# A two-layer conv and attention decoder on one core: raw x transposed first, its norm applied later

## The chip, the cores and the metric

The kernel runs on one core of one Trainium2 chip. The metric is device time in microseconds (us) of one execution, lower is better. The core has TensorE (PE, matmuls), VectorE (DVE), ScalarE (ACT), GpSimd (POOL) and SyncE (SP, which here only issues DMAs). Each works through a program of its own in order, and they wait for one another by semaphores.

## The reference

For S = 256 tokens and D = 1024 features, in float32:

```python
h = rmsnorm(x, norm_mix[0])              # y = x * rsqrt(mean(x*x) + EPS);  h = y * weight per feature
bg, cg, xv = split(h @ a_w_in, 3)        # three projections of 1024 columns
x = x + (bg * causal_conv3(cg * xv)) @ a_w_out
x = x + conv_ffn(rmsnorm(x, norm_ffn[0]))            # (silu(conv(h @ w_gate) + b) * (h @ w_up)) @ w_down, width 2816
k, v = split(rmsnorm(x, kv_norm) @ w_kv, 2)
x = x + attention(rmsnorm(x, norm_mix[1]) @ w_q, k, v) @ w_o
x = x + conv_ffn(rmsnorm(x, norm_ffn[1]))
out = rmsnorm(x, final_norm)
```

The convolution works along the tokens, feature by feature. The rms factor of a token (called rstd below) is one number per token, the norm weight one number per feature.

## The kernel before

All matrices are streamed once. A **slot** is 1 MB of weights, [128, 2048] in SBUF: 256 output columns for all 8 blocks k of 128 input features. SP loads slot s into one of six `raw` buffers (`load`), ACT rounds it to a high part (`hi(s)`), DVE subtracts to get the low part (`lo(s)`), and PE multiplies. A product is hi*hi + hi*lo + lo*hi. In the usual form (`project`) the weights are stationary and the tokens move: 16 matmuls of 512 columns (`both`: the high weight against the high and low part of h) and 16 of 256 columns (`narrow`: the low weight against the high part). The result lies by feature, in `main` and `cross` halves of a PSUM pair; ACT copies `cross` (`mixer_cross`), DVE adds `main` (`a_whole_sum`), and PE may then reuse that pair.

Slots 0 and 1 of the first projection hold 256 columns of C and 256 of x (`cg`, `xv`), slots 2 and 3 the next 256 of each, up to slot 7; four slots of B follow, then four of the output matrix. For each pair of slots DVE multiplies C by x and runs three taps on two blocks (`conv_a(i)`); later it multiplies by B (`gate_a`).

Before the change the beginning runs thus. SP loads x by token halves (tokens 0 to 127 in two pieces, tokens 128 to 255 in one), then slot 0 in halves, then slot 1. ACT squares x, DVE and POOL form rstd (POOL by a power), DVE multiplies x by rstd and by the norm weight that PE has spread over the partitions (`normalise`), PE transposes (`transposes`), ACT and DVE make hi and lo of it (`h_hi`, `h_lo`). Slots 0 and 1 are multiplied in another form, with the tokens stationary (`first_rows`): 8 k x 3 parts x 2 token halves x 2 slots = 96 matmuls of 256 columns. Their result lies by token, so it is copied (`copy_opening`) and turned by 8 transposes (`turn_opening`) within slot 2. `warm(n)` issues n matmuls whose result is not used.

Everything from slot 4 on is the same in both kernels, but for line numbers, counts of semaphores, and what GpSimd is given (below).

## Time and profile before

| | |
|---|---|
| median of 3 runs | 587.63 us (587.48 to 587.85) |
| the profiled execution | 587.62 us, span of its records 585.8 us |
| PE busy | 577.2 us, 99% of the span |
| DVE, ACT, POOL busy | 420.3, 314.9, 10.1 us |
| PE's share of the chain that ended last | 93% |

The span runs from the first record to the last; some 1.8 us lie around it. Busy time is a sum over instructions; matmuls overlap, so the time of one matmul in a stream is read from the spacing of the starts, or from the chain that ended last, where a group stands with its total and its count. Prefixes: L950 is line 950 of the kernel; PEld is the load of stationary data.

### The profile page before, as it was taken

What the parts mean: (1) busy time and instruction counts of PE and PEld (TensorE: products, weight loads), DVE (VectorE), ACT (ScalarE), POOL (GpSimd) and SP (SyncE); (2) the same over time, 40 slices, a digit from 0 to 9 for tenths busy, and PEclk for the clock granted to TensorE, in tenths of its full rate; (3) what the DMA queues carried; (4) which work ended last, traced back from release to release, by engine and by line L of the source; (5) the groups of instructions that cost most, each with busy time, mean ns of one, the idle gap of its engine ahead of it and who ended that gap; (6) DMA issues with size and microseconds to landing.
All of it is one profiled execution on the core that took longest, in us unless ns stands there. A gap on an engine that the chain in (4) does not pass through costs nothing.

```text
span 585.8 us, 8105 instructions
## 1 busy us (share of the span) xinstructions
PE 577.2 (99%) x3119; PEld 499.0 (85%) x3119; DVE 420.3 (72%) x508; ACT 314.9 (54%) x380; POOL 10.1 (2%) x22
## 2 busy tenths in 40 slices
PE   8999999999999999999999999999999999999995
PEld 6988888888888888888888899888888888888884
DVE  4688877767667667766886788896786667667765
ACT  5534453567544554555545666645665544554541
POOL 2000000000000000000100000000000000000001
PEclk9999999999999999999999999999999999999999
DMA  8995667456655655556654644274546655654001
GB/s 276 345 320 161 218 215 238 142 182 210 216 186 175 216 190 175 185 172 212 215 180 142 254 139 146 75 255 170 173 160 213 216 191 173 212 199 160 1 0 73
DMA packets 80917, 108.08 MB, mean 185 GB/s; under 512 B 1833, under 2 KB 71665, under 8 KB 80882
## 3 DMA queue, kind: packets, MB, share of 16 engines
q1 hardware_dynamic: 80160, 104.97, 54.2%
q10 hardware_dynamic: 722, 2.63, 1.2%
q8 instruction: 25, 0.41, 0.3%
q14 instruction: 10, 0.08, 0.0%
HBM read 106.54 MB, written 1.05 MB: 184 GB/s over the span
## 4 chain that ended last, share of the span: by engine, by line
PE 93%; DVE 3%; ACT 2%; DMA 1%; issue 1%; POOL 0%; SPq 0%; DVEq 0%; ACTq 0%
PE pair L950 36%; PE pair L958 19%; PE acc L1005 7%; PE acc L1009 7%; PE acc L1007 7%; PE pair L932 3%; PE pair L934 3%; PE pair L933 3%; PE acc L933 1%; PE acc L934 1%; PE acc L932 1%; PE pair L1019 1%; DMA xs<-in_x 1%; DVE wgt L617 1%; ACT acc L377 1%
## 5 line engine op out<-in xcount | busy, mean ns | idle before, releaser
L617 DVE TENSOR_TENSOR wgt<-raw,wgt 128x2048 fp32r<-128x2048 f32 x94 | 214.7, 2289 | 53.1 <-ACT wgt L359 52.8
L950 PE MATMUL pair<-hA,wgt 128*128 128x512 f32 x864 | 206.0, 391 | 0.0
L359 ACT ACTIVATE wgt<-raw 128x2048 fp32r<-128x2048 f32 x94 | 179.4, 1911 | 24.3 <-PE acc L1009 20.9
L950 PEld LDWEIGHTS pair<-hA,wgt 128*128 128x128 f32 x864 | 159.9, 188 | 31.8
L958 PEld LDWEIGHTS pair<-hA,wgt 128*128 128x128 f32 x864 | 108.0, 191 | 2.6
L958 PE MATMUL pair<-hA,wgt 128*128 128x256 f32 x864 | 108.8, 283 | 0.0
L1005 PE MATMUL acc<-wgt,kq_hi 128*128 128x512 f32 x160 | 49.3, 389 | 0.0
L1007 PE MATMUL acc<-wgt,kq_hi 128*128 128x512 f32 x160 | 49.3, 389 | 0.0
L1009 PE MATMUL acc<-wgt,kq_lo 128*128 128x512 f32 x160 | 49.2, 389 | 0.0
L427 ACT ACTIVATE scratch<-scratch 128x512 f32<-128x512 f32 x22 | 13.9, 632 | 59.7 <-DVE scratch L695 59.7
L441 ACT ACTIVATE scratch<-pair 128x512 f32<-128x512 f32 x20 | 11.9, 594 | 58.3 <-PE pair L958 58.3
L716 DVE TENSOR_TENSOR scratch<-scratch,pair 128x512 f32<-128x512 f32 x20 | 13.7, 686 | 31.0 <-ACT scratch L441 31.0
L1005 PEld LDWEIGHTS acc<-wgt,kq_hi 128*128 128x128 f32 x160 | 30.0, 188 | 6.2
L1007 PEld LDWEIGHTS acc<-wgt,kq_hi 128*128 128x128 f32 x160 | 30.0, 188 | 6.2
L1009 PEld LDWEIGHTS acc<-wgt,kq_lo 128*128 128x128 f32 x160 | 30.0, 188 | 6.2
L932 PE MATMUL pair<-wgt,hA 128*128 128x512 f32 (+1 forms) x96 | 34.7, 361 | 0.6 <-DVE wgt L831 0.6
L934 PE MATMUL pair<-wgt,hA 128*128 128x512 f32 (+1 forms) x96 | 34.0, 354 | 0.0
L933 PE MATMUL pair<-wgt,hA 128*128 128x512 f32 (+1 forms) x96 | 34.0, 354 | 0.0
L695 DVE SCALAR_TENSOR_TENSOR scratch<-scratch,f_par 128x255 f32<-128x255 f32 (+1 forms) x80 | 33.2, 477 | 0.0
L720 DVE TENSOR_TENSOR scratch<-scratch,pair 128x512 f32<-128x512 f32 x20 | 13.8, 688 | 23.7 <-ACT scratch L448 23.7
L377 ACT ACTIVATE acc<-xs 128x512 f32<-128x512 f32 x20 | 12.0, 602 | 28.4 <-DVE xs L628 24.9
L419 ACT ACTIVATE scratch<-scratch,f_par 128x256 f32<-128x256 f32 x40 | 21.6, 589 | 1.5 <-DVE scratch L716 1.5
(143 smaller groups left out, 583.3 us busy)
## 6 DMA issues: line engine op xcount, KB each, us to landing
raw<-in_ffn_w_up SPq DMA_DIRECT2D x44, 1024.0 KB, 5.1
raw<-in_ffn_w_down SPq DMA_DIRECT2D x22, 1024.0 KB, 4.9
raw<-in_a_w_in SPq DMA_DIRECT2D x11, 1024.0 KB, 10.6
raw<-in_w_kv SPq DMA_DIRECT2D x8, 1024.0 KB, 5.2
raw<-in_a_w_out SPq DMA_DIRECT2D x4, 1024.0 KB, 5.2
raw<-in_b_w_q SPq DMA_DIRECT2D x4, 1024.0 KB, 6.1
raw<-in_b_w_o SPq DMA_DIRECT2D x4, 1024.0 KB, 5.9
raw<-in_a_w_in SPq DMA_DIRECT2D x2, 512.0 KB, 7.2
```

The lines of the kernel that those rows point to most:

```text
L359: act.activation(split_slot(s)[0], raw[:, s % RAW, :], ACT.Copy).then_inc(w_hi_ready, 2 if s + 1 in AHEAD else 1)
L419: ins = act.activation(g[:, e, :], gate[:, e, :], ACT.Identity, bias=f_par[:, l, bass.ds(f + TAPS * FT, 1)], scale=f_par[:, l, bass.ds(f + ...
L617: dve.tensor_tensor(wlo, raw[:, s % RAW, :], whi.bitcast(F32), ALU.subtract).then_inc(w_lo_ready, 2 if s + 1 in AHEAD else 1)
L695: dve.scalar_tensor_tensor(out=dst, in0=gate[:, e, 0:S - back], scalar=f_par[:, l, bass.ds(f + (TAPS - 1 - back) * FT, 1)], in1=dst, op0=A ...
L932: pe.matmul(dst, sh, mh, start=first, stop=False)
L933: pe.matmul(dst, sh, ml, start=False, stop=False)
L934: return pe.matmul(dst, sl, mh, start=False, stop=last)
L950: last = pe.matmul(pair[b][:, e, :].rearrange("p (a n) -> p a n", a=2), whi[:, w], hid[:, :, k, :], start=first and k == 0, stop=not first ...
L958: last = pe.matmul(pair[b][:, e, 0:S], wlo[:, w], hid[:, 0, k, :], start=first and k == 0, stop=k == KD - 1)
L1005: pe.matmul(acc[t][h][:], ah, wh[h], start=first, stop=False)
L1007: pe.matmul(acc[t][h][:], ah, wl[h], start=False, stop=False)
L1009: last = pe.matmul(acc[t][h][:], al, wh[h], start=False, stop=False)
```

## The change

What it does, part by part:

- x is loaded by feature halves (all 256 tokens of features 0 to 511, then the rest) in two DMAs; slot 0 comes in quarters and slot 1 in halves, each with a semaphore of its own.
- PE transposes raw x. DVE multiplies the transposed x by the norm weight, now one number per partition (`scaled`), and ACT and DVE make hi and lo of that. The rms factor is not in it.
- The norm weight and the taps (32 rows) are loaded on ACT's DMA queue and turned by one small transpose; the FFN's parameters come between the halves of slot 1.
- rstd is spread: POOL makes rows of it, PE turns them (2 transposes), ACT copies them to `rstd_all`, POOL squares them. POOL then multiplies C by rstd squared (before the product with x), and the convolution's result by rstd, for each of four pairs: 8 POOL multiplies of 128x512.
- Slots 0 and 1 are multiplied in the usual form (`part_both`, `part_narrow`): 32 matmuls of 512 columns and 32 of 256. The copies and the 8 transposes of the opening are gone; the later warm-up is 6 instead of 8.

```diff
@@ loads (SP)
             for h in range(2):
-                sp.dma_start(xs[:, 0, 512 * h:512 * h + 512], x_rows[:, 0, 512 * h:512 * h + 512]).then_inc(x0_in[h], 16)
-            sp.dma_start(xs[:, 1, :], x_rows[:, 1, :]).then_inc(x1_in, 16)
-            halves = raw[:, 0, :].rearrange("p (g k n) -> p g k n", g=2, n=256)
-            for g, landing in enumerate((first_landed, landed[0])):
-                sp.dma_start(halves[:, g], in_rows[:, 4 * g:4 * g + 4, D:D + 256]).then_inc(landing, 16)
-            load(1, wide(in_rows, 2 * D))
+                sp.dma_start(xs[:, :, 512 * h:512 * h + 512], x_rows[:, :, 512 * h:512 * h + 512]).then_inc(x_in[h], 16)
+            quarters = raw[:, 0, :].rearrange("p (q k n) -> p q k n", q=4, n=256)
+            for q, landing in enumerate(first_landed + [landed[0]]):
+                sp.dma_start(quarters[:, q], in_rows[:, 2 * q:2 * q + 2, D:D + 256]).then_inc(landing, 16)
+            halves = raw[:, 1, :].rearrange("p (g k n) -> p g k n", g=2, n=256)
+            for g, landing in enumerate((second_landed, landed[1])):
+                sp.dma_start(halves[:, g], in_rows[:, 4 * g:4 * g + 4, 2 * D:2 * D + 256]).then_inc(landing, 16)
+                if g == 0:
...
             load(2, wide(in_rows, D + 256))
...
@@ GpSimd
+            for t in range(2):
+                root(0, t)
+                pool.wait_ge(rstd_ready, t + 1)
+                pool.tensor_scalar(rstd_rows[:, t, :], rstd_rows[:, t, :], rstd[:, t:t + 1], None,
+                                   ALU.mult).then_inc(rstd_rows_ready, 1)
+            pool.wait_ge(rstd_all_ready, 1)
+            pool.tensor_tensor(rstd_sq, rstd_all, rstd_all, ALU.mult).then_inc(rstd_sq_ready, 1)
+            pool.wait_ge(rstd_sq_ready, 1)
+            for i in range(KD // 2):
+                pool.wait_ge(a_sum, a_turn(i, 0))
+                c = a_whole[:, 0]
+                pool.tensor_tensor(c, c, rstd_sq.unsqueeze(1).to_broadcast([P, 2, S]), ALU.mult).then_inc(c_scaled, 1)
+                pool.wait_ge(a_conv_done, 2 * i + 2)
+                part = conv_out[:, 2 * i:2 * i + 2, :]
+                pool.tensor_tensor(part, part, rstd_all.unsqueeze(1).to_broadcast([P, 2, S]),
+                                   ALU.mult).then_inc(a_conv_scaled, 1)
...
-            root(0, 0)
-            root(0, 1)
@@ ScalarE
+            act.dma_start(par_rows[TAPS * KD:(TAPS + 1) * KD, 0, :],
+                          norm_mix[0].rearrange("(k n) -> k n", n=P)).then_inc(a_par_in, 16)
+            act.dma_start(par_rows[0:TAPS * KD, 0, :], a_conv[0].rearrange("t (k n) -> (t k) n", n=P)).then_inc(a_par_in, 16)
+            square(0, 0, 0)
+            square(0, 1, 0)
+            start_hi(0, 0)
+            start_hi(1, 0)
+            first_quarter_hi(0)
+            start_hi(0, 1)
+            first_quarter_hi(1)
+            start_hi(1, 1)
+            first_quarter_hi(2)
+            first_quarter_hi(3)
+            second_half_hi(0)
+            square(0, 0, 1)
+            second_half_hi(1)
+            square(0, 1, 1)
...
+            mixer_cross(0, 0)
+            hi(2)
+            act.wait_ge(rstd_T, 1)
+            act.activation(rstd_all, acc[0][0][:, 0:S], ACT.Copy).then_inc(rstd_all_ready, 1)
+            hi(3)
+            mixer_cross(0, 1)
+            hi(4)
@@ VectorE
+            def scaled(t, h):
+                dve.wait_ge(x_T, start_step(t, h))
+                weights = a_par[:, TAPS * KD + 4 * h:TAPS * KD + 4 * h + 4].unsqueeze(2).to_broadcast([P, 4, P])
+                dve.tensor_tensor(x_scaled[:, h, t], acc[t][h][:].rearrange("p (k n) -> p k n", k=4), weights,
+                                  ALU.mult).then_inc(normed_ready, 1)
...
+            dve.tensor_copy(a_par[:], pair[1][:, 0, 0:(TAPS + 1) * KD]).then_inc(a_par_ready, 1)
+            dve.wait_ge(a_par_ready, 1)
+            scaled(0, 0)
+            scaled(1, 0)
+            start_lo(0, 0)
+            scaled(0, 1)
+            start_lo(1, 0)
+            scaled(1, 1)
+            start_lo(0, 1)
+            start_lo(1, 1)
+            for q in range(4):
+                first_quarter_lo(q)
+            second_half_lo(0)
             mean_square(0, 0)
...
             mean_square(0, 1)
...
+            second_half_lo(1)
+            a_whole_sum(0, 0)
             lo(2)
...
+            a_whole_sum(0, 1)
+            conv_a(0)
             lo(4)
-            conv_a(0)
...
+                dve.wait_ge(a_sum, a_turn(i, 1))
+                dve.wait_ge(c_scaled, i + 1)
+                dve.tensor_tensor(cx, c_all, cx, ALU.mult).then_inc(cx_ready, 1)
@@ TensorE
+            R0, R1 = (TAPS + 1) * KD, (TAPS + 1) * FT
+            pe.wait_ge(a_par_in, 32)
+            pe.transpose(pair[1][:, 0, 0:R0], par_rows[0:R0, 0, :], ident[0:R0, 0:R0]).then_inc(a_par_T, 1)
+            for t, h in BY_HALF:
+                start_transposes(t, h)
+            warm(6)
+            for q in range(4):
+                if q % 2 == 0:
+                    for t in range(2):
+                        pe.wait_ge(h_lo_ready, start_step(t, q // 2))
+                pe.wait_ge(*((first_hi, q + 1) if q < 3 else (w_hi_ready, 1)))
+                part_both(0, 0, (2 * q, 2 * q + 1))
+            for q in range(4):
+                pe.wait_ge(*((first_lo, q + 1) if q < 3 else (w_lo_ready, 1)))
+                last = part_narrow(0, 0, (2 * q, 2 * q + 1))
+            last.then_inc(slot_done, 1)
+            for g in range(2):
+                pe.wait_ge(*((w_hi_ready, 2) if g else (second_hi, 1)))
+                part_both(1, 1, range(4 * g, 4 * g + 4))
+            pe.wait_ge(rstd_rows_ready, 2)
+            for t in range(2):
+                last = pe.transpose(acc[0][0][:, P * t:P * t + P], rstd_rows[:, t, :], ident[:])
+            last.then_inc(rstd_T, 1)
...
+            for g in range(2):
+                pe.wait_ge(*((w_lo_ready, 2) if g else (second_lo, 1)))
+                last = part_narrow(1, 1, range(4 * g, 4 * g + 4))
```

The order of PE's instructions at the beginning, before (the rows after the ones shown go on in threes up to 96; `x8` counts instructions):

```order
1 L1125 MATMUL acc<-ident 128x128 x4
2 L1130 MATMUL acc<-gain,ones 128x512 x2
3 L1019 MATMUL pair<-ident,scratch 128x128 x8
4 L1125 MATMUL acc<-ident 128x128 x8
5 L932 MATMUL pair<-wgt,hA 128x256
6 L933 MATMUL pair<-wgt,hA 128x256
```

and where slot 2 begins, with the opening's transposes (L1064) inside it:

```order
102 L1142 MATMUL acc<-ident,par_rows 128x24
103 L1144 MATMUL acc<-ident,par_rows 128x88 x2
104 L950 MATMUL pair<-hA,wgt 128x512 x8
105 L958 MATMUL pair<-hA,wgt 128x256 x8
106 L1064 MATMUL acc<-ident,scratch 128x128 x8
107 L950 MATMUL pair<-hA,wgt 128x512 x8
108 L958 MATMUL pair<-hA,wgt 128x256 x24
```

PE's whole beginning in the changed kernel, up to slot 2 (its first row is L1029 x16):

```order
1 L1213 MATMUL pair<-ident 128x128 x4
2 L1218 MATMUL pair<-ident,par_rows 128x32
3 L1050 MATMUL acc<-ident,xs 128x128 x16
4 L1213 MATMUL pair<-ident 128x128 x6
5 L1060 MATMUL pair<-hA,wgt 128x512 x16
6 L1069 MATMUL pair<-hA,wgt 128x256 x16
7 L1060 MATMUL pair<-hA,wgt 128x512 x16
8 L1237 MATMUL acc<-ident,rstd_rows 128x128 x2
9 L1241 MATMUL acc<-ident,par_rows 128x88 x2
10 L1069 MATMUL pair<-hA,wgt 128x256 x16
11 L1029 MATMUL pair<-hA,wgt 128x512 x16
```

All 16 transposes of x now stand ahead of the warm-up, which stands ahead of the first matmul; nothing but four small transposes interrupts the two slots. DVE's beginning before the change (L652 is `normalise`, L663 `h_lo`, L826 and L831 the low parts of slot 0):

```order
1 L632 TENSOR_SCALAR msq<-sumsq 128x1
2 L635 TENSOR_SCALAR msq<-sumsq,msq 128x1
3 L652 SCALAR_TENSOR_TENSOR scratch<-xs,rstd,acc 128x512 x2
4 L632 TENSOR_SCALAR msq<-sumsq 128x1
5 L635 TENSOR_SCALAR msq<-sumsq,msq 128x1
6 L826 TENSOR_TENSOR wgt<-raw,wgt 128x1024
7 L663 TENSOR_TENSOR hA<-pair,hA 128x4x128 x2
8 L652 SCALAR_TENSOR_TENSOR scratch<-xs,rstd,acc 128x512 x2
9 L831 TENSOR_TENSOR wgt<-raw,wgt 128x1024
```

and in the changed kernel (L874 is `scaled`, L880 `start_lo`, L886 and L892 the low parts of slots 0 and 1):

```order
1 L896 COPY a_par<-pair 128x32
2 L874 TENSOR_TENSOR scratch<-acc,a_par 128x512 x2
3 L880 TENSOR_TENSOR hA<-scratch,hA 128x4x128
4 L874 TENSOR_TENSOR scratch<-acc,a_par 128x512
5 L880 TENSOR_TENSOR hA<-scratch,hA 128x4x128
6 L874 TENSOR_TENSOR scratch<-acc,a_par 128x512
7 L880 TENSOR_TENSOR hA<-scratch,hA 128x4x128 x2
8 L886 TENSOR_TENSOR wgt<-raw,wgt 128x512 x4
9 L892 TENSOR_TENSOR wgt<-raw,wgt 128x1024
```

The norm's statistics are no longer ahead of anything here. The low part of the second token half of features 0 to 511 (row 5) stands behind a `scaled` that needs the second load of x (row 4).

## Rows read from the trace of the kernel before

**Rows 1.** The page: busy time, and the chain that ended last.

```profile
PE 577.2 (99%) x3119; PEld 499.0 (85%) x3119; DVE 420.3 (72%) x508; ACT 314.9 (54%) x380; POOL 10.1 (2%) x22
...
PE 93%; DVE 3%; ACT 2%; DMA 1%; issue 1%; POOL 0%; SPq 0%; DVEq 0%; ACTq 0%
```

**Rows 2.** PE's waits over the whole span: total, times, longest.

```profile
PE pair L932 <- DVE wgt L831: 0.6, 1, 0.6
```

**Rows 3.** PE and its loads, 0 to 14 us: start, length, what.

```profile
1.69 1.78 PEld L1125 LDWEIGHTS acc<-ident 128*128 128x128 f32 x8 [1.69 <-POOL ident L334]
...
7.40 0.71 PEld L1019 LDWEIGHTS pair<-ident,scratch 128*128 128x128 f32 x4 [1.50 <-DVE scratch L652]
...
9.01 2.93 PEld L1125 LDWEIGHTS acc<-ident 128*128 128x128 f32 x16
11.93 0.19 PEld L932 LDWEIGHTS pair<-wgt,hA 128*128 128x128 f32 x1
...
13.36 0.90 PEld L1019 LDWEIGHTS pair<-ident,scratch 128*128 128x128 f32 x8
```

**Rows 4.** The chain that ended last, in order of time: start, length, what.

```profile
1.64 5.84 DMA xs<-in_x
...
13.78 1.15 DVE wgt L831
...
15.06 0.36 PE pair L932
...
25.54 0.17 PE acc L1142
25.71 0.30 PE acc L1144 x2
26.01 1.88 PE pair L950 x8
...
28.85 0.87 PE acc L1064 x8
...
34.44 7.28 PE pair L950 x32
41.72 3.83 PE pair L958 x32
```

**Rows 5.** ACT's instructions, 0 to 24 us, with what ended its idle time.

```profile
4.52 0.60 ACT L377 ACTIVATE acc<-xs 128x512 f32<-128x512 f32 x1 [0.29 <-DMA xs<-in_x]
...
7.50 0.60 ACT L377 ACTIVATE acc<-xs 128x512 f32<-128x512 f32 x1 [2.25 <-DMA xs<-in_x]
...
13.47 1.91 ACT L359 ACTIVATE wgt<-raw 128x2048 fp32r<-128x2048 f32 x1 [1.54 <-DMA raw<-in_a_w_in]
...
16.66 1.92 ACT L359 ACTIVATE wgt<-raw 128x2048 fp32r<-128x2048 f32 x1 [0.30 <-DMA raw<-in_a_w_in]
20.09 1.92 ACT L359 ACTIVATE wgt<-raw 128x2048 fp32r<-128x2048 f32 x1 [1.52 <-DMA raw<-in_a_w_in]
```

**Rows 6.** The two halves of slot 0 (L290), from issue to landing.

```profile
L290 SPq DMA_DIRECT2D raw<-in_a_w_in x2: 434/470/507, 2.2 to 2.7; - x2
...
DMA to landing us min/median/max: 6.7/7.2/7.7
```

**Rows 7.** DVE in the first projection, 42 to 50 us.

```profile
42.82 2.29 DVE L617 TENSOR_TENSOR wgt<-raw,wgt 128x2048 fp32r<-128x2048 f32 x1
...
49.87 0.69 DVE L746 TENSOR_TENSOR gain<-gain,pair 128x512 f32<-128x512 f32 x1 [1.48 <-ACT gain L528]
```

**Rows 8.** DVE's busy time in a stretch of two slots.

```profile
38.00:49.10 11.10, 9.02 (x11) 1.00 0.73 235
```

**Rows 9.** POOL's instructions, 0 to 20 us.

```profile
1.34 0.29 POOL L334 TENSOR_SCALAR_AFFINE_SELECT ident<-ident 128x128 f32<-128x128 f32 x1 [0.24 <-POOL ones L332]
...
2.52 0.40 POOL L344 TENSOR_SCALAR_AFFINE_SELECT dist<-dist 128x256 f32<-128x256 f32 x1
5.58 0.55 POOL L328 TENSOR_TENSOR rstd<-msq,minus_half 128x1 f32<-128x1 f32 x1 [2.65 <-DVE msq L635]
```

More of the change, by code:

```diff
@@ L158, in build @@
         landed = [sem(f"landed{r}") for r in range(RAW)]
-        x0_in = [sem("x0_in_a"), sem("x0_in_b")]
-        x1_in = sem("x1_in")
+        x_in = [sem(f"x_in_{h}") for h in range(2)]
         gain_in = sem("gain_in")
-        gain0_spread = sem("gain0_spread")
         gained = sem("gained")
-        par_in = sem("par_in")
+        a_par_in = sem("a_par_in")
+        f_par_in = sem("f_par_in")
         consts = sem("consts")
@@ L240, in step4, with start_step @@
             return 4 * n + 2 * t + h + 1
+        def start_step(t, h):
+            return 2 * h + t + 1
+        BY_HALF = [(t, h) for h in range(2) for t in range(2)]
         def a_turn(i, b):
-            return 2 * (i - 1) + b + 1
+            return 2 * i + b + 1
         def f_turn(l, j, b):
@@ L501, in _ @@
-            for t in range(2):
-                for h in range(2):
-                    square(0, t, h)
-            first_half_hi()
-            for h in range(2):
-                h_hi(0, 0, h)
-            act.wait_ge(landed[0], 16)
-            act.activation(split_slot(0)[0][:, COLS // 2:], raw[:, 0, COLS // 2:], ACT.Copy).then_inc(w_hi_ready, 1)
-            hi(1)
-            for h in range(2):
-                h_hi(0, 1, h)
-            hi(2)
-            hi(3)
-            copy_opening(A_IN, 0, 0, 1)
@@ L515, in _, with first_quarter_hi @@
-            copy_opening(A_IN, 1, 0, None)
-            hi(4)
-            act.wait_ge(opening_T, 1)
-            act.activation(a_whole[:, 0], acc[0][0][:].rearrange("p (e n) -> p e n", e=2), ACT.Copy).then_inc(c_copied, 1)
+            def first_quarter_hi(q):
+                act.wait_ge(*((first_landed[q], 16) if q < 3 else (landed[0], 16)))
+                part = slice(q * COLS // 4, (q + 1) * COLS // 4)
+                act.activation(split_slot(0)[0][:, part], raw[:, 0, part],
+                               ACT.Copy).then_inc(first_hi if q < 3 else w_hi_ready, 1)
@@ new lines, in second_half_hi @@
+            def second_half_hi(g):
+                act.wait_ge(*((landed[1], 16) if g else (second_landed, 16)))
+                part = slice(g * COLS // 2, (g + 1) * COLS // 2)
+                act.activation(split_slot(1)[0][:, part], raw[:, 1, part],
+                               ACT.Copy).then_inc(w_hi_ready if g else second_hi, 1)
+            act.dma_start(par_rows[TAPS * KD:(TAPS + 1) * KD, 0, :],
+                          norm_mix[0].rearrange("(k n) -> k n", n=P)).then_inc(a_par_in, 16)
@@ L965, in project, with start_transposes, part_both, part_narrow @@
                 return last
[L967 to L981 removed]
+            def start_transposes(t, h):
+                pe.wait_ge(x_in[h], 16)
+                for k in range(4):
+                    last = pe.transpose(acc[t][h][:, P * k:P * k + P],
+                                        xs[:, t, 512 * h + P * k:512 * h + P * k + P], ident[:])
+                last.then_inc(x_T, 1)
+            def part_both(s, b, ks):
+                whi = split_slot(s)[0]
+                for e in range(2):
+                    for k in ks:
+                        w = slice(256 * k + P * e, 256 * k + P * e + P)
+                        pe.matmul(pair[b][:, e, :].rearrange("p (a n) -> p a n", a=2), whi[:, w], hA[:, :, k, :],
+                                  start=k == 0, stop=False)
+            def part_narrow(s, b, ks):
+                wlo = split_slot(s)[1]
+                for e in range(2):
+                    for k in ks:
+                        w = slice(256 * k + P * e, 256 * k + P * e + P)
+                        last = pe.matmul(pair[b][:, e, 0:S], wlo[:, w], hA[:, 0, k, :], start=False, stop=k == KD - 1)
                 return last
@@ L1124, in warm @@
                 for _ in range(count):
-                    pe.matmul(acc[0][1][:, 0:P], ident[:], ident[:], start=True, stop=True)
+                    pe.matmul(pair[1][:, 1, 0:P], ident[:], ident[:], start=True, stop=True)
             warm(4)
-            pe.wait_ge(gain_in, 16)
-            for h in range(2):
-                pe.matmul(acc[1][h][:], ones[:], gain[0:1, 512 * h:512 * h + 512],
-                          start=True, stop=True).then_inc(gain0_spread, 1)
-            transposes(0, 0)
@@ L1153, in _ @@
-            wide_slot(A_IN + 3, 1, hA)
-            for i in range(2, KD // 2):
+            last.then_inc(f_par_T, 1)
+            for g in range(2):
+                pe.wait_ge(*((w_lo_ready, 2) if g else (second_lo, 1)))
+                last = part_narrow(1, 1, range(4 * g, 4 * g + 4))
+            last.then_inc(slot_done, 1)
+            for i in range(1, KD // 2):
                 for b in range(2):
```

161 lines of the change are left out of this document (72 added, 89 removed).

## Prediction

> **What bounds the kernel now.** I read the page first. PE is busy for 577.2 of 585.8 us and holds 93% of the chain that ended last [rows 1], so this is a kernel of PE's stream. Then PE's waits: besides the wait for the identity matrix at the very start, its one wait of any size is 0.6 us for slot 0's second half [rows 2]. Busy time flatters the first microseconds, though, so I looked at what PE does there. Its first useful matmul starts at 11.93 us [rows 3]. The chain shows what precedes that region: x lands at 7.48 (1.64 + 5.84), then statistics and conversions, and the last of them ends at 14.93 [rows 4]. From 15.06 on the chain is PE's alone up to slot 4 and beyond. The kernel is therefore a start (until 11.93) and a stream, and whatever moves the beginning of slot 4 moves the end by as much, if nothing in between runs dry.
>
> Slot 4 begins in the middle of the group that starts at 34.44: that group is 16 matmuls of slot 3 and 16 of slot 4, so at 34.44 + 3.64 = 38.08 [rows 4]. From 11.93 to there are 26.15 us.
>
> **The stream, before and after.** In steady state a matmul of 512 columns costs 7.28/32 = 0.2275 us and one of 256 columns 3.83/32 = 0.120 [rows 4]. A slot in the usual form is 16 x 0.2275 + 16 x 0.120 = 5.56 us. Before, slots 0 and 1 took from 11.93 to 25.54 = 13.61 us, of which 96 x 0.120 = 11.5 are matmuls; the other 2.1 are transposes of x inside them (0.90 [rows 3]), the wait, and fills. Then come 0.47 for three small transposes (25.54 to 26.01), 0.87 for the 8 of the opening, and two slots (11.12): 26.1.
>
> After, the same distance is four slots, 4 x 5.56 = 22.24. To it are added two transposes of rstd at 0.11 (the 8 of L1064 took 0.87 [rows 4]), 0.22, and two of the FFN's parameters, 0.30 [rows 4]. For restarts at new semaphores I add 0.2. Sum 22.96. The stream shrinks by 26.15 - 22.96 = 3.2 us. The change of form itself gives only 0.38 of this (96 x 0.120 against 32 x 0.2275 + 32 x 0.120); the rest is what no longer stands between the matmuls.
>
> **When the stream starts.** Nothing waits for rstd any more. In PE's order the first matmul stands behind all 16 transposes of x, hence behind the second load of x, and behind `warm(6)`. When does that load land? The first 512 KB had landed at 4.52, the last at 7.48 [rows 4, 5]. At the rate of the first pieces (256 KB per 1.0 us) it would be 6.5; since slot 0's first packets no longer travel beside it, perhaps 6.0; as before it would be 7.5. I take 7.0. The first half's transposes are done by then. The other eight take 2 x 0.71 = 1.42 us [rows 3]: 8.45. `warm(6)` is 12 passes, since `warm(4)` shows 8; at that pace, 1.78/8 = 0.222 each [rows 3], 2.67 us: 11.1.
>
> That pace needs a word. The loads of the warm-up run at 0.222 apiece at 1.69 us, the later 16 in 2.93, i.e. 0.183, and from 11.93 on everything is at full pace: eight transposing loads take 0.90 at 13.36 where four took 0.71 at 7.40 [rows 3]. So TensorE was granted the lower of its two levels (1.2 GHz) for the first 11 us and rose to 2.4 during the second warm-up: n x 0.222 + (16 - n) x 0.111 = 2.93 gives n = 10.4, a rise at 11.3. The engine had been at work from 7.40 without a long gap before it rose. In the changed kernel it is at work from about 7.1, so I let the rise stay at 11.3. What PE does before it goes at half speed: whether it is warm-up or slot 0, it costs double. With the first matmul at 11.1, 0.1 us is lost.
>
> The start moves from 11.93 to 11.2 in full-speed terms: 0.7 us. With 3.2 that is 3.9 us. That the rise keeps its place is my choice; a later one and an earlier one are rivals below.
>
> **Is everything there in time?** Durations: a 512-column instruction is 0.69 us on DVE [rows 7] and 0.6 on ACT [rows 5]; a full slot is 2.29 on DVE [rows 7] and 1.91 on ACT [rows 5], quarters and halves in proportion.
> - h: x_T of the second half at 7.8 lets `scaled(0,1)` run to 8.6, `start_lo(1,0)` to 9.3, `scaled(1,1)` 10.0, `start_lo(0,1)` 10.7, `start_lo(1,1)` 11.4. Quarters 0 and 1 need the 9.3, quarter 2 the 11.4 but PE is there at 11.2 + 8 x 0.2275 = 13.0. Margin 1.6.
> - Slot 0: its halves landed at 2.2 + 6.7 = 8.9 and 2.7 + 7.7 = 10.4 [rows 6], so the quarters at about 8.1, 8.9, 9.7, 10.4, and ACT has the last rounded by 11.9. DVE's four low quarters end at 13.9; PE wants the first at 14.8 and the last at 16.3. Slot 0 ends at 16.8.
> - Slot 1: landed at 13.47 before [rows 5]; its halves are rounded at 13.0 and 14.9, wanted at 16.8 and 18.6. Low halves at 15.1 and 17.3, wanted at 21.0.
> - rstd: the last square ends at 15.7, statistics 16.1, POOL's power 0.55 [rows 9] and a row product of some 0.3 for the second half, 17.0; PE wants them at 20.5.
> - Slot 2: landed at 16.66 [rows 5], but ACT comes to it only after `mixer_cross(0,0)`, at 17.5: rounded 19.4, low part 21.7, wanted at 23.0. This is the thinnest margin, 1.3 us.
> - Slot 3: ACT first waits for the turned rstd (20.9), then rounds 21.3 to 23.2; low part 25.5, wanted at 28.6. `conv_a(0)` 26.2 to 29.6, slot 4's low part 31.9, wanted at 34.1.
>
> **What POOL does.** Eight multiplies of 128x512 that did not exist. No row shows one. From POOL's 0.29 for 128 and 0.40 for 256 elements the slope is 0.86 ns an element [rows 9]: from 0.6 us (0.40 + 0.22) to 1.0 (0.55 for the power of a single column, and 512 x 0.86 ns). I take 1.0, since it has two inputs like the power. C's product must fit between `a_whole_sum(i,0)`, which before ended near 45.8 (right behind the low part that ends at 45.11), and the product with x, which begins after 49.87 + 0.69 = 50.6 [rows 7]: 4.8 us, with one low part of 2.29 in them. It fits even when it runs after that. The convolution's product has a whole slot. If a POOL multiply stops DVE while it runs, that is 2.0 us per two slots; DVE has 11.10 - 9.02 = 2.1 us free there [rows 8], and it is ahead besides: slot 6's low part was ready at 45.11 [rows 7], and PE began slot 6 at 49.19 (41.72 + 3.83 + half of the next 7.28). So I cost it at nothing; its cover is these 2.1 us a pair and the 4.1 us lead. The Trainium skill (SBUF — State Buffer, SBUF: two separate sides) says that a DVE operation with two SBUF inputs and a GpSimd operation that reads SBUF shut one another out, and (GPSIMD Engine Reference, Engine selection) that GpSimd is about 2x slower on two inputs, which would be an estimate of 1.4 us. By that DVE would lack 0.7 us per pair, 2.8 in all, still inside the 4.1.
>
> **The sum.** 587.62 - 3.2 - 0.7 = 583.7; the profiled execution and the median agree within 0.01.
>
> **Rivals.**
> - *As worked out* (0.58): 583.7. Its own range is 582.9 to 584.4: the second half of x at 6.0 ends the warm-up at 10.1, and 1.2 us of slot 0 go at half speed, 10.7 in full-speed terms (583.2); at 7.5 the warm-up ends at 11.45 (583.9); restarts may cost 0 to 0.6.
> - *The clock rises late* (0.14). If it comes 3 us after my 11.3, PE does half the work in these 3 us and 1.5 are lost: 585.2. For it: the work ahead of the rise is of another kind now (16 transposes, then a shorter warm-up), and no row shows such a beginning. Against it: the three runs lie within 0.4 us, so the place of the rise repeats.
> - *Early clock* (0.08). The new beginning has real transposes from 4.6 instead of single-row matmuls, and the rise comes during the warm-up. Then warm(6) ends 1 us sooner and PE starts at about 9.9, and reaches slot 2 at 21.6, just when its low part is ready (21.7): 11.93 - 9.9 = 2.0 with the 3.2 gives 582.4.
> - *The feed binds* (0.12). The small transfers now ahead of slot 1's second half and of slot 2, or ACT's order, make slot 2's low part late. From 1.3 us of lateness on PE waits, one for one. At 2.5 late, 1.2 are lost: 584.9. For it: DMA was the releaser of ACT for slots 1 to 3 [rows 5].
> - *POOL takes the mixer over* (0.05), the slower side. Its place is the product of C ahead of `conv_a`, and DVE shut out during POOL's multiplies. It decides from (2.1 + 4.1/4)/2 = 1.6 us per multiply on. At 3 us: 4 x (6.0 - 2.1) - 4.1 = 11.5 us of PE waits against the 3.9 gained: 595.
> - *Nothing comes of it* (0.03): x's new access pattern lands it 3 to 4 us later than before, and all that was won is used up: 587.3.
>
> **The numbers.** A measurement of this kernel tells a difference from none at about 0.2%, 1.2 us. Faster by more: the first four cases, 0.92. Within: 0.03. Slower: 0.05. The range, 582.2 to 585.5, takes in the early and the late clock and the feed.
>
> **What would show it.** In the profile of the changed kernel: the first L1060 at about 11.1; the first matmul of slot 2 (L1029) at about 23.1 and no wait above 0.3 us ahead of it; slot 4 at 34.2 instead of 38.08; the POOL multiplies between 0.6 and 1.4 us and no wait of PE on DVE in the mixer. The prediction is wrong if x's second half lands after 9, if L1060 spacing stays at 0.43 beyond quarter 1, or if `conv_a` waits for POOL for longer than its slack.

## Result, and the profile after

The changed kernel takes 583.64 us (median of 6 runs, 583.20 to 584.77) against 587.86 (6 runs, 587.48 to 588.32): ratio 0.9933, 95% interval 0.9923 to 0.9944. Forecast were 583.7 in 582.2 to 585.5. The profiled execution took 584.41 us with a span of 582.6, 3.2 less than the 585.8 before.

The page of the changed kernel, beside [rows 1]: PE has 5.5 us less to do, and GpSimd 32 us more.

```profile
PE 571.7 (98%) x3073; PEld 494.7 (85%) x3073; DVE 422.9 (73%) x513; ACT 315.0 (54%) x383; POOL 42.0 (7%) x33
...
PE 91%; DVE 3%; ACT 1%; issue 1%; POOL 1%; DMA 1%; POOLq 0%; ACTq 0%; DVEq 0%
```

PE's waits, beside [rows 2]. The wait for slot 0 is gone; a new one of 1.6 us stands ahead of the transposes of rstd, and one of 1.0 ahead of the small transpose.

```profile
PE pair L1213 <- POOL ident L353: 1.8, 1, 1.8
PE acc L1237 <- POOL rstd_rows L359: 1.6, 1, 1.6
PE pair L1218 <- DMA par_rows<-in_a_conv: 1.0, 1, 1.0
```

PE's loads at the start, beside [rows 3], and the chain that ended last, beside [rows 4] (start, length, what; `...` marks pieces left out).

```profile
4.84 0.17 PEld L1218 LDWEIGHTS pair<-ident,par_rows 32*128 32x128 f32 x1 [1.25 <-DMA par_rows<-in_a_conv]
5.08 3.26 PEld L1050 LDWEIGHTS acc<-ident,xs 128*128 128x128 f32 x16
8.31 1.42 PEld L1213 LDWEIGHTS pair<-ident 128*128 128x128 f32 x12
9.66 1.69 PEld L1060 LDWEIGHTS pair<-hA,wgt 128*128 128x128 f32 x8
```

```profile
1.39 3.41 DMA par_rows<-in_a_conv
...
10.89 0.69 DVE hA L880
11.58 2.41 DVE wgt L886 x4
13.99 1.14 DVE wgt L892
...
16.24 1.27 POOL rstd_rows L359
17.51 0.55 POOL rstd L347
18.06 0.09 issue
18.15 2.78 POOL rstd_rows L359
20.93 0.04 issue
20.97 0.44 PE acc L1237 x2
21.41 0.15 PE acc L1241 x2
21.57 1.94 PE pair L1069 x16
23.51 3.65 PE pair L1029 x16
27.16 3.83 PE pair L1037 x32
31.00 7.28 PE pair L1029 x32
```

Slot 4 begins at 31.00 + 3.64 = 34.64 instead of 38.08, 3.44 us earlier; 0.2 of them are lost behind it, since the span is 3.2 shorter. The forecast was 34.2. But the way there differs: slot 0 began at 9.7, not at 11.1, since the second warm-up (12 loads in 1.42) already ran at the full pace, and 1.6 us were given back at the transposes of rstd, because GpSimd's second row product took 2.77 us. Was the forecast right by two errors that cancel? The experiments say: in this one execution, yes; in others, one or both are absent.

### The profile page after: what moved, and what is told of

Same layout as the page of the kernel before. It is cut to its first block, busy times and chain, and to the rows that moved or that the text cites. A ratio compares the mean times of both kernels' runs of the same rounds, so it can differ in the third digit from the quotient of the medians.

```text
span 582.6 us, 8036 instructions
## 1 busy us (share of the span) xinstructions
PE 571.7 (98%) x3073; PEld 494.7 (85%) x3073; DVE 422.9 (73%) x513; ACT 315.0 (54%) x383; POOL 42.0 (7%) x33
## 3 DMA queue, kind: packets, MB, share of 16 engines
q10 hardware_dynamic: 772, 2.64, 1.4%
## 4 chain that ended last, share of the span: by engine, by line
PE 91%; DVE 3%; ACT 1%; issue 1%; POOL 1%; DMA 1%; POOLq 0%; ACTq 0%; DVEq 0%
PE pair L1029 36%; PE pair L1037 19%; PE acc L1097 7%; PE acc L1095 7%; PE acc L1093 7%; PE pair L1011 3%; PE pair L1013 3%; PE pair L1012 3%; PE acc L1013 1%; PE acc L1012 1%; PE acc L1011 1%; PE pair L1107 1%; DVE wgt L673 1%; POOL rstd_rows L359 1%; DMA par_rows<-in_a_conv 1%
## 5 line engine op out<-in xcount | busy, mean ns | idle before, releaser
L1029 PE MATMUL pair<-hA,wgt 128*128 128x512 f32 x864 | 205.7, 391 | 0.0
L393 ACT ACTIVATE wgt<-raw 128x2048 fp32r<-128x2048 f32 x93 | 177.5, 1911 | 20.8 <-PE acc L1097 20.8
L1029 PEld LDWEIGHTS pair<-hA,wgt 128*128 128x128 f32 x864 | 160.0, 188 | 31.8
L347 POOL TENSOR_TENSOR rstd<-msq,minus_half 128x1 f32<-128x1 f32 x10 | 8.6, 856 | 516.6 <-DVE msq L691 516.6
L774 DVE TENSOR_TENSOR scratch<-scratch,pair 128x512 f32<-128x512 f32 x20 | 13.8, 688 | 23.7 <-ACT scratch L488 23.7
L1011 PE MATMUL pair<-wgt,hA 128*128 128x512 f32 x64 | 25.3, 396 | 0.0
L1013 PE MATMUL pair<-wgt,hA 128*128 128x512 f32 x64 | 25.0, 391 | 0.0
L1012 PE MATMUL pair<-wgt,hA 128*128 128x512 f32 x64 | 24.9, 390 | 0.0
L413 ACT ACTIVATE acc<-xs 128x512 f32<-128x512 f32 x16 | 9.6, 601 | 24.9 <-DVE xs L684 24.9
```

Of the source, the lines that this page charges most:

```text
L393: act.activation(split_slot(s)[0], raw[:, s % RAW, :], ACT.Copy).then_inc(w_hi_ready, 2 if s + 1 in AHEAD else 1)
L1011: pe.matmul(dst, sh, mh, start=first, stop=False)
L1012: pe.matmul(dst, sh, ml, start=False, stop=False)
L1013: return pe.matmul(dst, sl, mh, start=False, stop=last)
L1029: last = pe.matmul(pair[b][:, e, :].rearrange("p (a n) -> p a n", a=2), whi[:, w], hid[:, :, k, :], start=first and k == 0, stop=not first ...
```

## The experiments

Each kernel is the changed kernel but for the edit shown, unless the text says otherwise. Ratios are to the kernel before on the same chip. The experiments ran on three chips, and the changed kernel was run again on the first of them only, beside the next three experiments; for the others compare ratios, whose intervals are about 0.13% (0.8 us) to either side, or kernels that ran on one chip. By slot n I mean the beginning of its first matmul in the profile.

The beginning of slot 4 is a finer measure than the medians. In the profiles of the changed kernel and of its variants (all but the triple multiply), the execution's time less the beginning of slot 4 is 549.67 to 549.82 us, and 550.05 in one (rstd's transposes later). So what an edit does to its profiled execution can be read there to about 0.1 us, though one profile is one of several courses that a program can take.

**The changed kernel again.**

> The changed kernel once more, so that the others have a neighbour on the same chip. Both theories: 583.2 to 584.8, as in its six runs so far. The profile should again show a wait of PE of some 1.6 us ahead of the two transposes of rstd and a rise of the clock during the second warm-up.

583.42 us (582.93 to 584.86), ratio 0.9927 (0.9913 to 0.9940). Its profiled execution has no wait for rstd. PE's loads and the chain:

```profile
5.35 3.27 PEld L1050 LDWEIGHTS acc<-ident,xs 128*128 128x128 f32 x16
8.60 1.77 PEld L1213 LDWEIGHTS pair<-ident 128*128 128x128 f32 x12
```

```profile
10.57 3.67 PE pair L1060 x16
14.24 1.91 PE pair L1069 x16
16.15 3.66 PE pair L1060 x16
19.81 0.22 PE acc L1237 x2
20.02 0.15 PE acc L1241 x2
20.18 1.94 PE pair L1069 x16
22.12 3.65 PE pair L1029 x16
25.77 3.83 PE pair L1037 x32
29.60 7.28 PE pair L1029 x32
```

The warm-up took 1.77 instead of 1.42 us, so the clock rose in it; slot 0 begins at 10.57 and slot 4 at 33.24. From slot 0 to slot 4 are 22.67 us, where the forecast had 22.96. The same code has at least two courses, and this one, with the later start, is 1.4 us ahead at slot 4 (33.24 against 34.64). The repeat of the 1.6 us that was expected did not come: here GpSimd's second row product starts 0.22 us before VectorE's low part of slot 2 and takes 0.61.

**rstd's transposes later.**

```diff
@@ TensorE
-            pe.wait_ge(rstd_rows_ready, 2)
-            for t in range(2):
-                last = pe.transpose(acc[0][0][:, P * t:P * t + P], rstd_rows[:, t, :], ident[:])
-            last.then_inc(rstd_T, 1)
...
                 last = part_narrow(1, 1, range(4 * g, 4 * g + 4))
             last.then_inc(slot_done, 1)
+            pe.wait_ge(rstd_rows_ready, 2)
+            for t in range(2):
+                last = pe.transpose(acc[0][0][:, P * t:P * t + P], rstd_rows[:, t, :], ident[:])
+            last.then_inc(rstd_T, 1)
```

> PE's two transposes of rstd stand behind slot 1's last matmul instead of ahead of its narrow part; nothing else is changed. Theory A (GpSimd's spreading of rstd holds the stream up by 1.65 us): the wait moves to where GpSimd is long done, slot 4 begins at 33.0 instead of 34.6, time 582.0 to 582.4, about 1.6 below the changed kernel. Theory B (the start of the stream and the clock set the time, the wait only takes up slack in front of slot 2's low part): slot 2 then waits for that, and less than 0.6 us is won.

583.50 us (583.16 to 584.71), 0.9931 (0.9917 to 0.9944): nothing won in the median. Its profile has an early clock (12 loads in 1.46) and a row product of 2.72 us, as the changed kernel's, and no wait for rstd, but a new one (engine, operation, what ended the wait; the total, count and longest):

```profile
PE pair L1029 <- DVE gain L800: 0.4, 1, 0.4
```

ACT now waits longer for the turned rstd ahead of `hi(3)`; slot 3's low part, and behind it on VectorE `a_whole_sum(0,1)`, `conv_a(0)`, slot 4's low part and the next sum, all come later, and slot 4 begins at 33.45. Against the changed kernel's profile that is 1.2 us earlier: of the wait of 1.6, 0.4 came back by way of ACT's order. Its slow executions (584.47, 584.71) were not profiled, so why the median stays is not shown.

**rstd's rows on ScalarE.**

```diff
@@ GpSimd
                 root(0, t)
-                pool.wait_ge(rstd_ready, t + 1)
-                pool.tensor_scalar(rstd_rows[:, t, :], rstd_rows[:, t, :], rstd[:, t:t + 1], None,
-                                   ALU.mult).then_inc(rstd_rows_ready, 1)
@@ ScalarE
             hi(2)
+            for t in range(2):
+                act.wait_ge(rstd_ready, t + 1)
+                act.activation(rstd_rows[:, t, :], rstd_rows[:, t, :], ACT.Copy,
+                               scale=rstd[:, t:t + 1]).then_inc(rstd_rows_ready, 1)
```

> The two row products of rstd are made by ScalarE, after slot 2's high part, instead of by GpSimd; GpSimd keeps the powers and the eight multiplies. Theory A (GpSimd's row products took 1.27 and 2.77 us because VectorE's operations kept it out): on ScalarE each takes 0.3 us, PE's wait falls from 1.65 to under 0.3 and the time to 582.0 to 582.6. Theory B: within 0.6 us of the changed kernel.

583.86 us (583.04 to 583.93), 0.9926 (0.9912 to 0.9939). The two products took 0.68 us together and PE waits for rstd no more. Yet no time is won: here the clock rose late.

```profile
8.63 2.68 PEld L1214 LDWEIGHTS pair<-ident 128*128 128x128 f32 x12
11.19 3.57 PEld L1061 LDWEIGHTS pair<-hA,wgt 128*128 128x128 f32 x16
```

The whole warm-up at the low pace, 2.68 us (the forecast's 2.67), slot 0 at 11.5, slot 2 at 23.07, slot 4 at 34.19: this is the course that was predicted, to 0.1 us at slots 2 and 4. The edit is not needed for it: the kernel of the next experiment, which is the changed kernel up to GpSimd's multiplies, has it too, with the rows on GpSimd (12 loads in 2.64, row product 0.61, slot 4 at 34.13). Theory A alone does not stand: the wait for rstd costs time only where the start was early. The time is theory B's, but its reason, that the wait only takes up slack, is not right either, as the last experiments show.

**GpSimd's multiplies nearly empty.**

```diff
@@ GpSimd
-                pool.tensor_tensor(c, c, rstd_sq.unsqueeze(1).to_broadcast([P, 2, S]), ALU.mult).then_inc(c_scaled, 1)
+                pool.tensor_tensor(c[:, :, 0:1], c[:, :, 0:1], rstd_sq[:, 0:1].unsqueeze(1).to_broadcast([P, 2, 1]), ALU.mult).then_inc(c_scaled, 1)
...
-                pool.tensor_tensor(part, part, rstd_all.unsqueeze(1).to_broadcast([P, 2, S]),
+                pool.tensor_tensor(part[:, :, 0:1], part[:, :, 0:1], rstd_all[:, 0:1].unsqueeze(1).to_broadcast([P, 2, 1]),
```

> GpSimd's eight multiplies of 128x512 are cut to 128x2 each, so the scaling by the norm factor is left out for all but one column; waits and semaphores stay. Theory A (they are hidden, though they take 3.3 us beside VectorE): the time is that of the changed kernel within 0.3 us, VectorE's low part right after the first product falls from 2.79 to 2.29. Theory C (the multiplies cost PE time somewhere in the mixer): 1 us or more is won.

583.88 us (583.16 to 584.85), 0.9932 (0.9918 to 0.9946): the eight multiplies cost nothing. The scaling is left out for all but two columns, yet GpSimd still waits for VectorE: a multiply of 128x2 takes 2.2 us where VectorE's low part is running, and 0.19 where it is not.

```profile
32.46 2.18 POOL L367 TENSOR_TENSOR gain<-gain,rstd_rows 128x2 f32<-128x2 f32 x1 [0.62 <-DVE gain L800]
41.83 0.19 POOL L367 TENSOR_TENSOR gain<-gain,rstd_rows 128x2 f32<-128x2 f32 x1 [0.62 <-DVE gain L800]
```

So the edit removes GpSimd's work and not its waits; that neither delays PE follows from PE's waits in both profiles, of which none lies in the mixer. VectorE's low part is 2.28 us here (at 32.30) and 2.79 in the changed kernel, as expected.

**A longer warm-up** (`warm(12)` for `warm(6)`).

> The second warm-up is 12 matmuls instead of 6. Theory S (the stream begins behind the warm-up, and everything behind it follows rigidly): 12 more loads at 0.11 us begin slot 0 some 1.2 us later, so 584.5 to 585.0 with a first matmul of slot 0 at 11.6 to 12.7. Theory F (VectorE's chain of low parts and statistics sets slot 2, the start has slack): less than 0.4 us above the changed kernel.

584.49 us (583.98 to 585.57), 0.9949 (0.9937 to 0.9961): 1.1 us above the changed kernel's 583.42, which is of another chip, so the medians alone do not show it clearly. The profile does: slot 0 begins at 12.28 and slot 4 at 34.94, both 1.7 us later than in the repeat (10.57, 33.24), and nothing waits between them. The stream follows its start rigidly.

**No second warm-up** (`warm(6)` taken out).

> No second warm-up. Theory S: the first matmul of slot 0 comes when the low parts of the first feature half are there, about 9.8 us, in every execution; where the clock rises only at 11.3 the first matmuls run at half pace but do useful work. 582.6 to 583.0, and a smaller spread between executions than the 1.9 us of the changed kernel. Theory F: no change. A third possibility: without the warm-up the clock rises later, 584 or more.

584.64 us (584.17 to 584.95), 0.9952 (0.9939 to 0.9966): slower by 1.2 than the changed kernel on another chip and by 0.9 than the kernel with the loads as before (583.79) on the same one, the third possibility. The spread is small, the time is bad. The chain:

```profile
9.74 5.70 PE pair L1060 x16
15.44 1.91 PE pair L1069 x16
```

The first matmul came at 9.74, as theory S had it. But PE's loads pause from 8.4 to 9.7, and then 16 matmuls of 512 columns took 5.70 us instead of 3.65: 2.05 us more than at the full pace, which is half of what was spent at 1.2 GHz, so the clock rose near 13.8. Slot 4 begins at 34.44, 1.2 later than in the repeat. So the warm-up is no waste; it stands where PE must wait for h anyway.

**The norm first again.** The stream's form, the loads and the order stay, only the factor is applied before the transposes.

```diff
@@ ScalarE
-            square(0, 0, 0)
-            square(0, 1, 0)
+            for t, h in BY_HALF:
+                square(0, t, h)
             start_hi(0, 0)
@@ VectorE
+            mean_square(0, 0)
+            mean_square(0, 1)
+            for t, h in BY_HALF:
+                dve.wait_ge(rstd_ready, t + 1)
+                dve.tensor_scalar(early[:, t, 512 * h:512 * h + 512], xs[:, t, 512 * h:512 * h + 512], rstd[:, t:t + 1],
+                                  None, ALU.mult).then_inc(early_ready, 1)
             scaled(0, 0)
@@ TensorE
-                pe.wait_ge(x_in[h], 16)
+                pe.wait_ge(early_ready, start_step(t, h))
...
-                                        xs[:, t, 512 * h + P * k:512 * h + P * k + P], ident[:])
+                                        early[:, t, 512 * h + P * k:512 * h + P * k + P], ident[:])
@@ GpSimd
-                pool.wait_ge(rstd_ready, t + 1)
-                pool.tensor_scalar(rstd_rows[:, t, :], rstd_rows[:, t, :], rstd[:, t:t + 1], None,
+                pool.tensor_scalar(rstd_rows[:, t, :], rstd_rows[:, t, :], 1.0, None,
```

(The later squares and statistics are gone from their places; `early` is a raw buffer that slot 5 fills later; SP waits for the transposes before it.)

> The norm factor is applied before the transposes again (four products on VectorE, after both halves of x, all squares and the power), everything else is as in the changed kernel, and GpSimd's multiplies are by ones. Theory S: the transposes begin near 11 us instead of 5.4, slot 0 near 15, and the stream loses 3.5 to 4.5 us: 587 to 588, no better than the kernel before. If only the new form and the missing transposes counted, it would stay below 585.

586.97 us (11 runs, 586.73 to 587.80), 0.9994 (0.9985 to 1.0003): not told from the kernel before, and 3.3 above the changed kernel. PE waits where it had worked:

```profile
PE acc L1055 <- DVE raw L903: 3.4, 1, 3.4
```

The transposes begin at 8.7 and slot 0 at 13.96, later than the 11.93 of the kernel before [rows 3]; slot 4 comes at 37.06. From slot 0 to slot 4 it takes 23.1 us, against the 26.15 before, so slot 4 is 1.0 earlier than before in these two profiles. This is not the old beginning with a new stream: since x comes by feature halves, the norm here waits for all of x, where the kernel before could begin on its first token half. The usual form behind the old beginning by token halves was not run.

**The loads of the weights as before** (slot 0 in halves, slot 1 whole).

> Slot 0 is loaded in halves and slot 1 whole, as before; the conversions in quarters and halves stay. Slot 0's first half lands at 8.9 us against 8.1 for a quarter, slot 1 at 13.5, so its high part's halves are ready at 14.5 and 16.4, wanted at 16 and 18. Theory S: no change, within 0.4 us of the changed kernel. If the splitting into quarters matters: 0.6 us or more slower.

583.79 us (583.45 to 584.63), 0.9934 (0.9921 to 0.9947), within 0.4 of the changed kernel: splitting the loads brings nothing that can be measured. Its profile is another with the early clock (12 loads in 1.57) and the row product held up (2.72 us), and slot 4 at 34.89:

```profile
PE acc L1235 <- POOL rstd_rows L357: 1.7, 1, 1.7
```

**Three multiplies for one on C.**

```diff
@@ GpSimd
+                for again in range(2):
+                    pool.tensor_tensor(c, c, rstd_sq.unsqueeze(1).to_broadcast([P, 2, S]), ALU.mult).then_inc(spare_done, 1)
+                    pool.wait_ge(spare_done, 2 * i + again + 1)
                 pool.tensor_tensor(c, c, rstd_sq.unsqueeze(1).to_broadcast([P, 2, S]), ALU.mult).then_inc(c_scaled, 1)
```

> Of each pair, C is multiplied by rstd squared three times on GpSimd instead of once (so C, and the output, carry a wrong power of the factor), one multiply waiting for the last. One multiply took 1.30 us alone and 3.34 beside VectorE's low part. The prediction's rival put the point from which GpSimd decides at 1.6 us per multiply held against VectorE. Theory L (GpSimd waits for VectorE more than VectorE for it): two more multiplies of about 1.3 to 1.7 us delay conv_a by 2 to 3 us a pair, against a lead of VectorE of 4: PE waits under 1.5 us in all, 583.5 to 585. Theory M (each multiply of GpSimd costs VectorE its length): 6 us a pair against some 2 free, PE waits 8 us or more, 592.

589.88 us (588.95 to 590.43), 1.0036 (1.0022 to 1.0049): slower than the kernel before, by more than theory L allows and less than M. GpSimd, start and length (the groups of two are the two added multiplies):

```profile
31.91 3.26 POOL L374 TENSOR_TENSOR scratch<-scratch,dist 128x512 f32<-128x512 f32 x1 [3.61 <-DVE scratch L822]
35.13 4.72 POOL L369 TENSOR_TENSOR gain<-gain,rstd_rows 128x512 f32<-128x512 f32 x2
39.93 1.29 POOL L371 TENSOR_TENSOR gain<-gain,rstd_rows 128x512 f32<-128x512 f32 x1
44.83 3.26 POOL L374 TENSOR_TENSOR scratch<-scratch,dist 128x512 f32<-128x512 f32 x1 [3.61 <-DVE scratch L822]
```

There is a loop: the convolution's product (3.26), C's products (6.1), then VectorE's product and taps (3.6), which release the convolution's product again: 12.92 us (31.91 to 44.83) for a pair whose matmuls take 11.12. Neither engine is busy all the time; the ring of waits is what is too long. PE waits 5.1 us in all. In the changed kernel the same ring takes 10.19 us (30.19 to 40.38), and VectorE's product waits in it for GpSimd:

```profile
30.19 3.28 POOL L370 TENSOR_TENSOR scratch<-scratch,dist 128x512 f32<-128x512 f32 x1 [6.28 <-DVE scratch L818]
33.44 3.34 POOL L367 TENSOR_TENSOR gain<-gain,rstd_rows 128x512 f32<-128x512 f32 x1
36.88 0.69 DVE L808 TENSOR_TENSOR gain<-gain 128x512 f32<-128x512 f32 x1 [0.66 <-POOL gain L367]
```

**Filling PE in the kernel before.**

```diff
@@ TensorE, kernel before
                           start=True, stop=True).then_inc(gain0_spread, 1)
+            warm(3)
             transposes(0, 0)
```

> The kernel before with three more warm-up matmuls between the spread of the norm weight and the first transposes, so that PE has no gap from 6.1 to 7.4 us and the clock may rise earlier, as in the changed kernel. Theory S2 (in the kernel before the first matmul waits for the low part of h, so an earlier clock is worth nothing; only in the changed kernel does the warm-up stand in the way): 587.5 to 588.1, no change. If the clock is what the change won: 586.5 or less.

587.86 us (11 runs, 587.03 to 588.26), 1.0004 (0.9995 to 1.0013). It did not test what it was meant to: PE's loads show no gap to be filled (the two matmuls of 512 columns ahead of it last until 7.4), the warm-up pushed the transposes to 8.63, and the clock did not rise earlier. What it shows is that the kernel before can bear its transposes 1.2 us later at next to no cost: the two slots end at 25.64, against 25.54 [rows 4]. Whether an earlier clock would have helped that kernel stays open.

**A first warm-up that reaches to the transposes, with rstd's rows on ScalarE** (`warm(7)` for `warm(4)`, and the edit of the experiment of that name).

> The changed kernel with 7 instead of 4 matmuls in the first warm-up, which fills PE's gap from 3.6 to 4.9 us ahead of the small transpose, and with rstd's rows made on ScalarE. If PE's work without a gap brings the rise of the clock forward, it lies at or below 8.5 us in most executions, slot 0 begins at 9.7, no wait for rstd follows: slot 2 at 21.9, 582.2 to 582.8 and a spread under 1 us. If the rise does not move: 583.2 to 584, as the changed kernel.

582.84 us (582.37 to 582.87), 0.9916 (0.9902 to 0.9929). The lowest median of all, 0.8% below the kernel before. It is 0.6 to 0.8 us below the changed kernel's (583.42 and 583.64), but on another chip, and the intervals of the ratios overlap. Clearer is the spread: 0.5 us, where the changed kernel has 1.9 (582.93 to 584.86 in 11 executions). PE's loads at the start, start and length:

```profile
1.81 3.06 PEld L1214 LDWEIGHTS pair<-ident 128*128 128x128 f32 x14 [1.81 <-POOL ident L353]
5.09 0.18 PEld L1219 LDWEIGHTS pair<-ident,par_rows 32*128 32x128 f32 x1 [0.23 <-issue]
5.33 2.57 PEld L1051 LDWEIGHTS acc<-ident,xs 128*128 128x128 f32 x16
7.87 1.42 PEld L1214 LDWEIGHTS pair<-ident 128*128 128x128 f32 x12
9.93 1.68 PEld L1061 LDWEIGHTS pair<-hA,wgt 128*128 128x128 f32 x8 [0.64 <-DVE hA L881]
```

The 16 transposing loads take 2.57 instead of 3.27: the rise falls into them. Slot 0 begins at 9.96, when h is there, and slot 4 at 33.05, only 0.2 earlier than in the repeat of the changed kernel: what the edit brings is the changed kernel's good course, every time.

**The same with rstd's rows on GpSimd.**

> As the last, but with rstd's rows on GpSimd, as in the changed kernel. If the rise comes early, slot 0 begins at 9.7 and GpSimd's second row product meets VectorE's low part of slot 2, 2.77 us instead of 0.61: PE waits 1.6 us, and the time stays at 583.2 to 584.4. If the row product finds its gap, 582.5, as with the rows on ScalarE.

584.45 us (584.24 to 584.68), 0.9945 (0.9932 to 0.9959). The early clock is there as well (16 loads in 2.00), but the row product meets VectorE's low part of slot 2: both start at 18.21.

```profile
16.31 1.27 POOL L359 TENSOR_SCALAR rstd_rows<-rstd_rows,rstd 128x128 f32<-128x128 f32 x1
17.54 0.57 POOL L347 TENSOR_TENSOR rstd<-msq,minus_half 128x1 f32<-128x1 f32 x1
18.21 2.72 POOL L359 TENSOR_SCALAR rstd_rows<-rstd_rows,rstd 128x128 f32<-128x128 f32 x1
```

```profile
18.21 2.32 DVE L673 TENSOR_TENSOR wgt<-raw,wgt 128x2048 fp32r<-128x2048 f32 x1 [0.53 <-ACT wgt L393]
```

PE waits 1.6 us in the profile, and the five times (584.24 to 584.68) leave no room for an execution without the wait. The last kernel ran on the same chip, and all its times lie below 582.9: the 1.6 us between the medians are what GpSimd's two small products cost when the start is early. An earlier start alone did not make the kernel faster; its median is 1.0 above the changed kernel's 583.42 on another chip, with intervals of the ratios that just overlap.

## Why the prediction was right, point by point

- **The stream** (3.2 us). Right. From slot 0 to slot 4 the changed kernel takes 22.67 us where nothing waits (forecast 22.96; only the 0.2 for restarts was too much, and the small transposes cost 0.37, not 0.52).
- **The start** (0.7 us). The mechanism was right: the end of the second warm-up sets it, shown by `warm(12)`, which moves slot 4 by 1.7 us; with the earliest clock h is ready at about the same time (9.7). Its place is not one number. The warm-up's 12 loads took 1.42, 1.46, 1.57, 1.77, 2.64, 2.68 and 2.68 us in seven profiled executions whose programs are the same up to there on PE, so slot 0 begins between 9.7 and 11.5; the forecast's 11.1 lies near the late end. "I let the rise stay at 11.3" is the step that did not hold: the rise moves from execution to execution. What the argument from the three runs' agreement missed is that the kernel before cannot show it: once begun, its matmuls still wait for the second half of slot 0's low part, which ends at 14.93 [rows 4], and a delay of its transposes by 1.2 us cost 0.1 there.
- **The early-clock rival** (0.08, 582.4). Its condition came about in the profiled execution, and its time did not: 584.4. It did not reckon with rstd.
- **When x lands.** Taken as 7.0. Its second half landed at 6.5 (issued at 1.2, 5.3 us to landing), and PE never waited for it: the 16 loads of the transposes follow one another without a gap in 3.26 us from 5.08, and the last end at 8.34. That this is near the forecast's 8.45 is luck, since PE's pace sets it (16 loads at 0.204) and not x's landing with eight loads behind it. That the first could not begin before 5.08, because the norm weight's small transpose ahead of them waited for its DMA (landed at 4.80), was not foreseen. It cost 0.2 us, and 0.5 in the repeat (5.35), x's first half being there at 4.84; the chain that ended last begins with this DMA in both.
- **rstd in time** (17.0, wanted at 20.5). This term was mis-sized. Behind the statistics the forecast had one power and one row product of 0.3 us; there are two of each in a row, and a row product took 0.61 alone and 1.27 to 2.77 beside VectorE. From 15.60 that made 5.3 us, and the rows were ready at 20.93 in the changed kernel's profile; in the repeat it was 3.2 us, and they were ready at 19.02. What decides is the second row product. VectorE's low part of slot 2 starts when ACT has rounded slot 2, and ACT comes to that when slot 0 is multiplied: the earlier slot 0, the earlier the low part. In the four profiles with the rows on GpSimd and 12 loads in 1.57 us or less (one of them with `warm(7)`), the two start within 0.03 us of one another and the product takes 2.72 to 2.77; where the loads took 1.77 or more it starts first and takes 0.61. The sign named beforehand, no wait above 0.3 us ahead of slot 2, fails in the first of these courses and holds in the other. So an early clock gives back more than it has won: slot 4 at 34.64 and 34.89, against 34.13 with a late clock and 33.24 between. That is why the two errors of the profiled execution nearly cancelled: not luck alone, the one calls up the other. That the median agrees with the forecast to 0.06 us is luck, as the six times lie over 1.6 us.
- **The spread** of 1.9 us (11 executions). With the rows on ScalarE it is 0.9, and 0.5 with `warm(7)` as well, so both the rise and the row product seem to have a part. That the three executions of the changed kernel above 584.4 all have the long row product is shown for the profiled one alone.
- **Slot 2's low part** as the thinnest margin: no run waited for it.
- **GpSimd's multiplies at nothing.** Right in the sum (emptied: no gain), the cover wrongly named. A multiply takes 1.30 us alone (forecast 1.0) and up to 3.37 with VectorE in the way; by the signs named beforehand it was to be 0.6 to 1.4. The prediction counted how long VectorE might be held, with 2.1 us a pair and a lead of 4.1 as cover. The cover that counts is that of the ring of waits: 3.28 + 3.37 + 3.6 = 10.3 us (`conv_a` starts at 26.70, 36.88 and 47.15), against 11.12 for PE's two slots. 0.8 us a pair is left, no more. The slower rival's place was right, its point of 1.6 us per multiply was not: it goes by the two multiplies with their waiting, 7.5 us together.
- **The rule on the shared port.** The Trainium skill (SBUF — State Buffer, SBUF: two separate sides) has whoever starts first keep the other out for the whole instruction. The traces agree, with one exception: a row product that starts with VectorE's low part takes 2.72 us, 0.61 without; the low part of 2.79 us begins while a GpSimd multiply has still 0.6 us to run, and is 2.29 otherwise. The exception is in the repeat, where the low part starts at 18.63, with 0.4 us of the row product still to run, and is 2.29 all the same. The estimate of 1.4 us for a multiply, from the Trainium skill's GPSIMD Engine Reference, Engine selection, was nearer to the 1.30 than the 1.0 from rows.
- **Deferring the norm** is the core. Undone by itself it takes back 3.3 of the 4.2 us, though the stream stays 3 us shorter (23.1 against 26.15): transposes and norm are then in front of slot 0, which begins 2.0 us later than in the kernel before. With x loaded by feature halves, the short stream pays only because the factor no longer delays its start. What splitting the loads brings is under what can be measured. The change of the matmuls' form was not tried alone, nor behind the old beginning by token halves, so how much of the gain could be had without deferring the norm stays open.

What stays open: why the clock rises where it does in a given execution. Only that it came earlier with more of PE's work ahead of it (`warm(7)`, two profiles), and later with a gap (no second warm-up, one profile), was seen.

## What to carry to other kernels

A factor that is the same along a contraction can be applied behind the matmuls; ask what the start of the stream then waits for next, and whether the engine that applies it is kept out by a neighbour. Where a stream starts before TensorE's clock has risen, fill the gaps ahead of it with matmuls, but no longer than the data takes, and look at what an earlier start then meets: here it did not pay until GpSimd's two small products were moved. If an engine gets work that is "hidden", add up the whole ring of waits through it and compare that with the period, not its busy time with the others' idle time.

## What was not expected of the hardware

- GpSimd's multiply of 128x512 with two inputs: 1.30 us alone, 3.28 to 3.37 beside VectorE's operations on two SBUF inputs; its row product of 128x128 0.61 and 2.72 to 2.77. Even a multiply of 128x2 takes 2.2 us there, and 0.19 without.
- The instant at which the clock rises differs between executions of one program: the same 12 loads took 1.42 and 1.77 us, and 1.46 to 2.68 with edits that come only after them on PE.
- Without the second warm-up, with PE idle from 8.4 to 9.7, the first 16 matmuls of 512 columns took 5.70 us instead of 3.65: the start was as early as in the changed kernel's profile (9.7), and the clock cost 2 us.
